# Regrouping the order of a token mixer's steps in a two-layer diffusion step on one Trainium2 core

## The reference

```python
sh1, sc1, g1, sh2, sc2, g2 = split(silu(c) @ ada_w[l] + ada_b[l], 6)      # the "ada" matmuls
h = rmsnorm(x, norm1_g) * (1 + sc1) + sh1
da_q, da_k, da_v, mb_z, mb_xbc, mb_dt, ml_q, ml_k, ml_v, ml_o, ml_if = split_columns(h @ w_in)
y_da = differential attention(q, k, v)             # 4 heads, softmax over context and latent keys
y_mb = rmsnorm(ssd_scan(conv(xbc), dt) * silu(z))  # Mamba-2, both directions
y_ml = rmsnorm(mlstm(q, k, v, i, f)) * sigmoid(o)  # chunkwise mLSTM, both directions
gates = sigmoid(h @ w_mgate + b_mgate)             # 3 x 1024 channels
merged = sum over the 3 branches of gates[n] * (y_n @ w_branch[n])
x = x + g1 * (merged @ w_out)
h = rmsnorm(x, norm2_g) * (1 + sc2) + sh2
x = x + g2 * expert_choice_ffn(h)                  # 16 SwiGLU experts of 1024 x 1024 x 3
```

## Time and profile before

| | |
|---|---|
| median of 3 runs | 2181.73 us (2176.8 to 2193.53) |
| the profiled execution | 2182.11 us |
| its span, first to last instruction | 2180.3 us |
| PE busy | 1932.8 us, 89% |
| DVE busy | 676.4 us, 31% |
| ACT busy | 378.1 us, 17% |
| mean granted clock of TensorE | 0.958 |
| HBM, mean over the span | 250 GB/s |

### The profile page before, as it was taken

One profiled execution on the slowest core, in us unless ns is written; L12 is line 12 of the kernel. 1 busy time (PEld: TensorE's weight loads), 2 busy tenths in 40 slices (PEclk: granted clock), 3 DMA queues, 4 the chain that ended last, 5 costly groups with the idle time before them and its releaser, 6 DMA issues. The chain is left out here.

```text
span 2180.3 us, 21734 instructions
## 1 busy us (share of the span) xinstructions
PE 1932.8 (89%) x8224; PEld 1000.7 (46%) x8224; DVE 676.4 (31%) x1740; ACT 378.1 (17%) x891; POOL 37.9 (2%) x68
## 2 busy tenths in 40 slices
PE   6988899899999999998899888988999898989887
PEld 2544455446554343434354445544555444343433
DVE  1212334335343323232122124245353323232312
ACT  2122321212211011111121123112231111010101
POOL 0000000000000000000000000000000000000000
PEclk9999899899989999999999899999999899999999
DMA  8323223230569999999962332332217599999995
GB/s 344 125 86 128 82 101 139 78 139 21 230 274 398 427 426 428 427 428 427 426 234 94 130 116 85 121 116 78 101 61 306 232 421 427 427 428 428 428 427 241
DMA packets 81655, 547.05 MB, mean 251 GB/s; under 512 B 6992, under 2 KB 10064, under 8 KB 50704
## 3 DMA queue, kind: packets, MB, share of 16 engines
q1 hardware_dynamic: 79104, 536.76, 60.6%
q0 software_dynamic: 2016, 8.06, 1.0%
...
HBM read 541.97 MB, written 3.67 MB: 250 GB/s over the span
## 5 line engine op out<-in xcount | busy, mean ns | idle before, releaser
L836 PE MATMUL bank_D<-HM,ring 128*128 128x384 f32 x1600 | 562.4, 509 | 44.4 <-ACT arena_b L1341 16.7
L836 PEld LDWEIGHTS bank_D<-HM,ring 128*128 128x128 f32 x1600 | 311.4, 199 | 266.2 <-issue 77.3
L1281 PE MATMUL bank_D<-ring,HM 128*64 128x512 f32 x912 | 207.8, 603 | 9.1 <-ACT HM L1609 6.6
L842 PE MATMUL bank_D<-ring,HM 128*128 128x512 f32 x384 | 172.1, 603 | 7.0 <-ACT ring L1431 7.0
L1281 PEld LDWEIGHTS bank_D<-ring,HM 128*64 128x64 f32 x912 | 77.7, 139 | 128.0 <-issue 118.8
L999 PE MATMUL bank_D<-arena_c,ring 128*128 128x384 f32 x384 | 130.5, 501 | 4.7 <-issue 4.7
L842 PEld LDWEIGHTS bank_D<-ring,HM 128*128 128x128 f32 x384 | 72.6, 193 | 93.4 <-issue 92.2
L2197 DVE TENSOR_TENSOR EB<-EB,bank_D 128x512 f32<-128x512 f32 x32 | 22.0, 688 | 266.7 <-ACT EB L1621 266.7
L1305 PE MATMUL bank_Y<-ring,EB 128*64 128x512 f32 x432 | 99.0, 603 | 4.7 <-issue 4.7
L999 PEld LDWEIGHTS bank_D<-arena_c,ring 128*128 128x128 f32 x384 | 74.4, 196 | 56.8 <-issue 10.4
L2209 DVE COPY arena_b<-bank_Y 32x512 f32<-32x512 f32 x64 | 44.1, 689 | 173.6 <-PE bank_Y L1305 173.1
...
## 6 DMA issues: line engine op xcount, KB each, us to landing
ring<-ex_w_gate SPq DMA_DIRECT2D x32, 2048.0 KB, 21.5
ring<-ex_w_down SPq DMA_DIRECT2D x27, 2048.0 KB, 26.9
ring<-ex_w_up SPq DMA_DIRECT2D x25, 2048.0 KB, 18.6
ring<-ada_w SPq DMA_DIRECT2D x23, 2048.0 KB, 7.7
arena_a<-ex_w_down SPq DMA_DIRECT2D x20, 2048.0 KB, 22.1
ring<-w_in SPq DMA_DIRECT2D x16, 2048.0 KB, 10.0
ring<-w_mgate SPq DMA_DIRECT2D x12, 2048.0 KB, 9.1
arena_a<-ex_w_up SPq DMA_DIRECT2D x12, 2048.0 KB, 22.6
```

The source lines that it names most:

```text
L836: last = mm(u.t[:, 0:N], w[:, kt, c * P:(c + 1) * P], src[:, kt, :], start=kt == 0, stop=kt == KT - 1)
L842: last = mm(u.t[:, :], HT[:, kt, tile(t)], w[:, kt, 0:CH], start=kt == 0, stop=kt == KT - 1)
L1281: last = mm(u.t[64 * c:64 * c + 64, :], XE[:, h * 4 + k, j, :], w[:, k, c * 512:(c + 1) * 512], start=h == 0 and k == 0, stop=h == 1 and k ...
```

## The change

The function `schedule` is written anew, with a table `PLACED` that says behind which step an ada chunk stands, and with four tables that say how many dense units each call of `take` places. `MIX_CHUNKS` and `last_use` are derived from the list of steps. Except for the wait of `out 0` no instruction of any engine is added, removed or altered; their order is. In the lists, in short (`a4` is ada 4, `at1` is ada_turn 1, `gn.d` is gate n d):

In `take_late` the ada chunks 8, 9 and 10 now count as units of their own (they hold back and flush like dense units); 4 to 7 and 11 don't. The diff, cut to its core:

```diff
-MIX_CHUNKS = (
-    [("q", Q0), ("k", K0), ("v", V0), ("z", Z0), ("ada", 4), ("x0", X0), ("ada", 5), ("x1", X0 + CH), ("ada", 6)]
...
+FILL_SCORE = (1, 1, 1, 1, 0, 1, 2, 1, 1, 1, 1, 1, 1, 0)
+FILL_TURN = (0, 0, 0, 0, 0, 0, 1, 0, 0, 1, 0, 0, 1, 0)
+FILL_MAMBA = (1, 0, 0, 1, 0, 1, 1, 0, 1, 0, 1, 1, 0, 0, 1, 1, 2, 0, 0, 1, 1, 1, 0, 0, 0)
+FILL_MLSTM = (0, 0, 0, 1, 1, 1, 0, 1, 1, 0, 1, 0, 0, 1, 1, 1, 0, 0, 0, 0, 1)
+PLACED = {("q", 1): [("ada", 4)],
+          ("k", 1): [("ada", 5)],
+          ("v", 1): [("ada", 6)],
+          ("merge", 0, 4): [("ada_turn", 1)],
+          ("mq", 3): [("ada", 8), ("ada", 9)],
+          ("merge", 1, 7): [("ada", 11)],
+          ("gate", 2, 0): [("ada_turn", 2)],
+          ("merge", 0, 3): [("ada", 7)],
+          ("mv", 2): [("ada", 10)]}
...
+    def add(*steps):
+        for step in steps:
+            s.append(step)
+            for more in PLACED.get(step, []):
+                if more[0] == "ada" and step[0] not in ("q", "k", "v", "merge"):
+                    fillers.append([more])
+                s.append(more)
 
     def take(k=1):
         for _ in range(k):
-            if dense:
-                fillers.append([step for step in dense[0] if step[0] not in ("ada", "ada_turn")])
-                s.extend(dense.pop(0))
-
-                if len(fillers) > 1 and fillers[-2][0][0] in fold:
-                    s.append(fold[fillers[-2][0][0]])
+            if not dense:
+                return
+            step = dense.pop(0)
+            fillers.append([step])
+            add(step)
+            for short, fold in (("dt", "dt_fold"), ("if", "if_fold")):
+                if (short,) in s and step != (short,) and (fold,) not in s:
+                    s.append((fold,))
+            if step in (("dt",), ("if",)):
+                take()
...
+MIX_STEPS = {}
+for _step in SCHEDULES[0][0]:
+    if mix_chunk_of(_step):
+        MIX_STEPS[mix_chunk_of(_step)] = MIX_STEPS.get(mix_chunk_of(_step), []) + [_step]
+MIX_CHUNKS = list(MIX_STEPS)
...
+def last_use(key):
+    return MIX_STEPS[key][-1]
...
-                        pe.wait_ge(h_ready, ready + (kt + 1))
+                        pe.wait_ge(ready[0], ready[1] + (kt + 1))
...
-                    pe.wait_ge(merged, l * 16 + 16)
                     pe.wait_ge(u.drained, u.before)
-                    to_channels(u, w, d % 4, MG)
+                    to_channels(u, w, d % 4, MG, (merged, l * 16 + 8) if d == 0 else None)
```

More of the change, by code:

```diff
@@ L119, in schedule @@
-    s += [("z_sig",)]
-    dense += [[("mq", j)] + ([("ada", 8)] if j == 3 else []) for j in range(4)] + [[("if",)]]
-    dense += [[("gate", 1, d)] + {3: [("ada", 9)], 7: [("ada", 10)]}.get(d, []) for d in range(KT)]
-    dense += [[("mv", t)] for t in range(TT)]
-    take()
-    s += [("acum",)]
-    take()
+        add(("merge", 0, d), *([("conv_out", d - 1)] if 1 <= d <= 6 else []))
+    dense += [("mq", j) for j in range(4)] + [("if",)] + [("gate", 1, d) for d in range(KT)] + [("mv", t) for t in range(TT)]
@@ L152, in schedule @@
+        take(next(fill))
+    add(("mb_gain", TT - 1))
     take(len(dense))
-    s += [("mb_gain", TT - 1), ("y_turn", 1, TT - 1)]
+    add(("y_turn", 1, TT - 1))
     for d in range(KT):
-        s += [("merge", 1, d)]
+        add(("merge", 1, d))
         if small and d % 2:
-            s += small.pop(0)
-    for x in small:
-        s += x
-    dense += [[("mo", t)] + ([("ada", 11)] if t == TT - 1 else []) for t in range(TT)]
-    dense += [[("gate", 2, d)] + ([("ada_turn", 2)] if d == 0 else []) for d in range(KT)]
@@ L163, in schedule @@
-    s += [("k_turn", t) for t in range(TT)]
-    take()
+            add(small.pop(0))
+    dense += [("mo", t) for t in range(TT)] + [("gate", 2, d) for d in range(KT)]
+    fill = iter(FILL_MLSTM)
+    for t in range(TT):
+        add(("k_turn", t))
+        take(next(fill))
     for i in range(4):
-        s += [("cstate", i)]
-        if i < 2:
-            take()
-    s += [("mo_sig",)]
+        add(("cstate", i))
+        take(next(fill))
+    add(("mo_sig",))
     for t in range(TT + 1):
@@ L189, in schedule @@
+    add(*[("merge", 2, d) for d in range(KT)])
+    more = layer + 1 < DEPTH
     for d in range(KT):
-        s += [("out", d)]
+        add(("out", d))
         if d == 0:
-            s += [("sh_row",), ("rb",)]
+            add(("sh_row",), ("rb",))
         if d == 1:
-            s += [("sh_perm",), ("rb_fold",)]
+            add(("sh_perm",), ("rb_fold",))
         if 0 < d < KT - 1:
-            s += [("x_turn", d - 1)]
+            add(("x_turn", d - 1))
         if d == KT - 2:
-            s += [("router", 0)]
```

149 lines of the change are left out of this document (74 added, 75 removed).

## The result

| | before | after |
|---|---|---|
| median | 2186.35 us (2176.8 to 2193.53, 4 runs) | 2076.26 us (2075.64 to 2076.52, 4 runs) |
| ratio to before, 95% interval | | 0.950 (0.946 to 0.954) |
| span of the profiled execution | 2180.3 us | 2074.7 us |
| mean granted clock over the span | 0.958 | 0.980 |

The kernel became 110 us faster by the medians and 105.6 us by the two spans. The prediction was 2089, 93 less than the profiled execution of before; the time lies in its range and the direction is right.

The account below looks back on a forecast made before the run. The prediction took the mixers as bound by one in-order PE queue with holes and a lowered clock; the experts' DMA-bound stretch only moves. Gains of 50.9 us in layer 0 and some 42 in layer 1 gave 2182.1 - 93 = 2089 us, range 2058 to 2138.

Parts of the forecast that it names:

- The holes: PE's idle waits in layer 0's mixer: 18.5 us gained in attention, 12.1 Mamba, 2.5 and 2.1 mLSTM, 0.6 lost at states.
- the places of the ada chunks: Attention: with ada 4 to 6 among q, k, v, the waits of x0, x4, gate0.0 and gate0.4 go.
- DVE's order at turn3 and turn9: Attention: DVE's other work comes first, so PE waits 2.1 us before turn3 and 3.1 before turn9.
- the slot of gate2's weights: States: gate2's load needs ada8's slot and 8.1 us; PE arrives after 6.1, so gate1.0 waits 2.0 us.
- The predicted places of the mLSTM's first half: mo0, mo1, mo2 between the cstates remove two waits; idle 4.5 becomes 2.0 us, 5.1 gained with the clock.
- those of its second half: mLSTM's second half: waits of 0.45 at num0.1, 1.3 at num2.1, 0.7 at y_turn2.1 replace 4.6 us; 2.1 gained.
- the rival of the late weights: Mixer loads landing in 20.7 us would make PE wait 58.6 us a layer: 2202 us, slower; chance 0.05.
- the rival that it would not: Small groups around the fillers keep the clock low; only idle time counts, 36.0 us a layer: 2110 us; chance 0.22.
- the prediction's terms of the clock: Layer 0's mixer: full clock returns behind removed waits, 5.5 us in attention, 7.4 in Mamba, part of 3.6 in mLSTM's first half.
- The bound by the granted clock: Upper bound, missing clock share times stage time: 16.4 us attention, 1.6 states, 7.4 Mamba, 6.0 mLSTM's first half.
- Layer 1's 9.2 us: Layer 1's mixer: PE was busy 9.2 us less, which can't be given back, so 50.9 becomes some 42.
- out0's wait: After the last merge: waiting for one merged tile at a time removes 1.41 us of idle time.

Follow-up runs that it names:

- the run of ada 4 to 6 alone: Kernel before with only ada chunks 4 to 6 and their loads moved among q, k and v, attention's fillers otherwise left: 2145.11 us, ratio 0.982.
- the kept filler: Changed kernel with mv2 and ada10 one place earlier, ahead of diag2.1, so nothing is kept between off2.1 and y_turn1.2: 2092.72 us, ratio 0.958.
- the three mended kernels: Changed kernel, one edit each: x unit to score4 and att_y0 behind turn5; conv0 behind turn9; ada8, ada9, `if` and gate1.0 moved: 2065.24, 2064.28, 2070.07 us.
- the run with the filled holes: Changed kernel plus matmuls without use, three ahead of turn3, four ahead of turn9, three ahead of gate1.0: 2068.74 us, ratio 0.9475.

## Why the prediction was right, and where it was off

**The holes.** This was the main step, and it held to 1.2 us. For layer 0 the prediction's terms without the clock and without out0 are 18.5 - 0.6 + 12.1 + 2.5 + 2.1 = 34.6 us of idle time; between the first q unit and the end of the last merge it fell from 54.2 to 20.8, by 33.4. The single holes: turn3 2.35 (2.1 predicted), x3 1.38 (1.1), turn9 3.48 (3.1), state3 1.39 (1.4), gate1.0 2.23 (2.0), decay0.1 0.98 and 0.32 (1.2), ada11 1.11 (1.2). Most of these causes were then shown by moving them: the places of the ada chunks by the run of ada 4 to 6 alone, the kept filler by taking it away, DVE's order at turn3 and turn9 and the slot of gate2's weights by the three mended kernels. The predicted places of the mLSTM's first half were tested only by moving ada11; those of its second half by no run.

**The weights.** gate2's load was issued when ada8 ended:

```profile
289.18 2.08 SPq L705 DMA_DIRECT2D ring<-w_mgate  x2
```

gate1.0 began at 297.13, 7.95 us later, where 8.1 was taken. The rule of the Trainium skill (DMA: Bandwidth & Descriptors, Anatomy of one DMA) that the prediction set beside it, 2.0 us and bytes over 436 GB/s, gives, as an estimate, 6.8 us for this 2 MB load; it is stated for the gpsimd path, and on SP's queue the trace does not agree with it. No other wait on DMA appeared in either mixer behind q0 (layer 1's gate1.0 waited 2.70), so the rival of the late weights is out.

**The clock: right mechanism, term too small.** The clock came back, so the rival that it would not is out, and the run with the filled holes shows the cause at turn3 and turn9; at gate1.0 it fits, and mq1 has another. The size was off. For layer 0 the prediction's terms of the clock are 5.5 - 0.6 + 7.4 + 2.6 = 14.9 us; PE's busy time fell by 486.6 - 464.05 = 22.5. The mis-sized term is the count in attention and the mLSTM: it went by the units of L836 and a little for "the small groups around them". By lines, over layer 0's mixer, the units to channels gave back 9.1 us (239.6 to 230.5), tokens and merges 4.6, and the small products and transposes nearly all of the remaining 8.8. By stages, for the same steps, it fell by 10.9 us in attention (ada7, which left it, counted back), where the terms had 5.5, by 6.7 from the states to the last merge of Mamba, where they had 6.8, and by 5.0 in the mLSTM, where they had 2.6. The bound by the granted clock, which the prediction had as well, was the better measure: it gave 16.4 + 1.6 + 7.4 + 6.0 = 31.4 us lost before, and by the same rule 0.03 x 107.3 + 0.07 x 48.5 = 6.6 are lost after, so 24.8 given back.

**Layer 1's 9.2 us: true of one execution, not of the layer.** The prediction subtracted them because PE was busy for less time in layer 1 of the profiled execution. Against that execution the subtraction was of the right kind: PE's busy time fell by 10.4 us in layer 1 (477.3 to 467.0), where 14.9 - 9.2 = 5.7 were forecast, and by 22.5 in layer 0. But another execution of the same mixer order had 486.4 us there, as layer 0 has. The granted clock differs from execution to execution, and with it the time of the kernel before: over all its runs 2173 to 2194 us, with a mean granted clock of 0.965 in the fastest and 0.952 in the slowest. Layer 1 thus gained 44.2 us against the profiled execution (40.3 predicted without out0) and 53.2 against the other. This also says why the medians differ by 110 and the spans by 105.6: the profiled execution of before (2182.1) lay 4 us under the median.

**q0 and out0.** The first q unit came 2.45 us earlier in the profiled execution of after; no order explains that, since other executions with this order of loads began as late as 37.9. out0's wait is gone from its row, as predicted (no idle time at 520.17). Whether its 1.4 us a layer reach the end is open for layer 0, where the stretch behind the merge did not get shorter; that the weights' stream starts at the merge and not at out0 would explain it, but this was only argued.

**What the prediction did not see.** mq1 at 7.12 us. The prediction looked for low clocks behind holes; this one stands behind 5.3 us of small products and transposes (acum to b_turn1), and of the 16 units in the eight profiles with this order 14 were slow (7.12 to 7.75). The rival said that small groups may pull the clock down as before. At this one place they did, though not at the others.

**Where the total comes from.** By spans: 2.45 (q0's start) + 56.0 (layer 0's mixer 55.8, the stretch behind it 0.2) + 44.2 (layer 1's mixer) + 2.9 behind the last merge = 105.6. The sum said 49.5 + 40.3 + 2.8 = 93. The 13 between them are 6.5 in layer 0, which the clock's term makes up, 3.9 in layer 1, where the clock gave 4.7 more than forecast and the holes 0.8 less, and q0's 2.45, which came with the two executions. One sum of the prediction doesn't come out: the items that it names for the lower end of its range give 2 x (4.2 + 6.7) + 5 = 27 below 2089, that is 2062 and not 2058; the measured time lies above both.
